# Two attentions in which one VectorE instruction adds the bias and keeps the row maximum

## The chip, the cores and the metric

The kernel runs on one core of a Trainium2 chip. The core has a matrix engine (TensorE, PE in the profile), a vector engine (VectorE, DVE), an activation engine (ScalarE, ACT), a general one (GpSimd, POOL) and SyncE (SP), which here issues loads. Each has its own queue of instructions, which it runs in order; they meet at semaphores. Data lie in SBUF; matrix products go to PSUM, here used as four banks of 128x512 (`BANK`) and two pairs of banks (`PAIR`). The metric is device time in microseconds (us).

## The reference, cut to what matters

The program is two two-layer blocks, one behind the other, for 512 tokens of width 1024. Each has an attention with 8 heads of width 64:

```python
# first block: the bias goes by the distance of query and key
scores = jnp.einsum('bclhd,bcshd->bchls', q, k_band).astype(jnp.float32) * (ATT_HEAD_DIM ** -0.5)
scores = scores + bias[None, None]
scores = jnp.where(valid[None, :, None, None, :], scores, -1e30)
p = jax.nn.softmax(scores, axis=-1).astype(v.dtype)
o = jnp.einsum('bchls,bcshd->bclhd', p, v_band)
...
# second block: normed queries and keys, a bias from the forget gates, causal
q = rms_norm(q, q_gain)
k = rms_norm(k, k_gain)
...
s = jnp.einsum('bqhd,bkhd->bhqk', qi, k).astype(jnp.float32) * scale
s = s + ci.transpose(0, 2, 1)[..., None] - ck[:, :, None, :]
s = jnp.where(kpos[None, :] <= pi[:, None], s, NEG_INF)
pr = jax.nn.softmax(s, axis=-1)
```

A softmax needs the largest score of each row, which is taken from the scores after scale and bias.

## The kernel before, in words

The whole program is one sequence per engine, written out by hand in `pe_program`, `dve_program`, `act_program`, `pool_program` and the loads of SP. No scheduler moves anything; semaphores (`bank_ready`, `bank_free`, `evac` and those of a stage) carry what depends on what. Layer normalisations, projections, two mixtures of experts, a state-space layer, an S5 layer and two feed-forward layers stand around the attentions; for their products POOL splits each weight into a high and a low part (`WH`, `WL`), and the PE runs three products.

Both attentions are the same three functions, `pe_attention`, `dve_attention` and `act_attention`; `n` is 0 for the first and 1 for the second, which the profile shows at some 190 and 1540 us. A head's scores are four row blocks `j` of 128 queries, with 128, 256, 384 and 512 keys, and lie in three banks (`HOME`). For a head `h`:

- PE, `scores(h)` (L1336, in the second attention with a product for the gates' bias, L1339): four products into three banks, each of which must have been handed back by the DVE.
- DVE, `scale(h)` (L1390): for each of the four blocks one instruction, scores times one eighth plus bias, from PSUM to `S`; the bank is handed back. Then four maxima (L1395), and their negation (L1397), which lets ACT begin.
- ACT, `exponential(h)` (L1448): four exponentials with the negated maximum as bias, and the rows' sums by the accumulator.
- DVE, `normalise(h)` (L1401, L1404): reciprocals of the sums, four products in place.
- PE, `turned(h)` (L1355): ten transposes of the probabilities; ACT copies them to `PT` (L1465); PE, `outputs(h)` (L1368): four products with V.

The DVE runs scale(0), scale(1), and then for each head normalise(h), other work, scale(h + 2). The other work is in the first attention two pieces of a matrix-vector product (`dve_ada`, L630 to L634) on weights that SP loads into `ADA_B`, and in the second `dve_s5_turning` (L3253 to L3255). Every other head it also takes the low part of two heads' outputs (`rest`, L1410). The PE runs turned(h), scores(h + 2), outputs(h). The projection behind an attention begins when the last low part is there.

The copies of the queries out of the projection are `act_copy_pairs` in the first attention, and `dve_qknorm` (L2725, with the gains `QK_GAIN`) makes those of the second; `MINUS_HEAD` is a constant with which the gates' bias is added in the PE.

## Time and profile before

| | us |
|---|---|
| median of 3 runs | 2767.97 (2766.33 to 2770.85) |
| profiled execution | 2766.05 |
| its span | 2764.1 |
| PE busy | 2495.0 (90%) |
| DVE busy | 1801.5 (65%) |
| POOL busy | 1469.9 (53%) |
| ACT busy | 964.4 (35%) |
| the 64 additions of both attentions (L1390) | 280 to 690 ns each |
| the 64 maxima (L1395) | 285 to 677 ns each |

The span is the time from the first to the last instruction of the profiled execution; the device time is a little longer. "Busy" counts the time in which an engine has at least one instruction in work. In a timeline the first number is the start in the span, the second the duration, and square brackets hold the idle time in front of it and who ended it; rows of the same line that follow one another are merged, with their count. The duration of a single instruction includes a tail in which the next one may already run, so the distance of two starts is less than the duration.

### The profile page before, as it was taken

The numbers are of one execution on the slowest core, as the hardware profiler recorded it, in microseconds if no ns is written. First come the engines' busy times: TensorE is split into PE (matmuls) and PEld (weight loads), VectorE is DVE, ScalarE is ACT, GpSimd is POOL, SyncE is SP. The second block draws the span as 40 slices with busy tenths as digits, with TensorE's granted clock in tenths as the row PEclk, the third lists the DMA queues.
The fourth block names the chain that finished last, engine by engine and source line by source line (L and its number), as shares of the span: only waits on it lengthen the run. The fifth ranks groups of instructions, "written<-read, shape, count | busy, mean of one in ns | idle before, by whom it ended". The sixth has DMA issues, their size and how long they took to land.

```text
span 2764.1 us, 36708 instructions
## 1 busy us (share of the span) xinstructions
PE 2495.0 (90%) x12718; PEld 1986.0 (72%) x12718; DVE 1801.5 (65%) x2200; ACT 964.4 (35%) x1494; POOL 1469.9 (53%) x1234
## 2 busy tenths in 40 slices
PE   4978989978999998999497789999996889999998
PEld 3754777856777776878386558888885778888887
DVE  6769866757787875667687857665137945666324
ACT  2013257742444432777312323222014631222102
POOL 4730334426555552344365126676779937666675
PEclk8977989989999998999798789999998999999999
DMA  8735569953333323899432113332241023333222
GB/s 312 261 131 205 190 241 331 325 176 92 99 99 93 98 83 116 282 337 311 141 81 80 65 54 92 105 93 89 98 125 47 32 67 94 91 103 95 95 88 84
DMA packets 319122, 386.73 MB, mean 140 GB/s; under 512 B 51578, under 2 KB 259214, under 8 KB 318902
## 3 DMA queue, kind: packets, MB, share of 16 engines
q1 hardware_dynamic: 261424, 335.84, 37.1%
q10 hardware_dynamic: 34438, 28.08, 3.3%
q0 software_dynamic: 23168, 21.59, 2.4%
q8 instruction: 57, 0.93, 0.1%
q14 instruction: 35, 0.29, 0.0%
HBM read 397.62 MB, written 55.41 MB: 164 GB/s over the span
## 4 chain that ended last, share of the span: by engine, by line
PE 35%; POOL 20%; issue 18%; DVE 14%; DMA 9%; ACT 2%; SPq 0%; ACTq 0%; POOLq 0%; DVEq 0%
POOL WL L837 14%; PE PAIR L529 6%; PE PAIR L530 5%; PE PAIR L531 5%; POOL WH L833 5%; PE PAIR L1842 4%; PE BANK L529 2%; PE BANK L530 2%; PE BANK L531 2%; DMA RAW<-in_ffn_w_up 2%; DMA RAW<-in_moe_w 2%; PE PAIR L1812 2%; DVE ADA_SUM L634 1%; PE BANK L2288 1%; DVE ADA_SUM L632 1%
## 5 line engine op out<-in xcount | busy, mean ns | idle before, releaser
L837 POOL TENSOR_TENSOR WL<-RAW,WH 128x512 fp32r<-128x512 f32 x584 | 815.1, 1426 | 12.2
L529 PE MATMUL PAIR<-HH,WH 128*128 128x512 f32 x1792 | 712.5, 398 | 56.1 <-POOL HL L1126 29.9
L530 PE MATMUL PAIR<-HL,WH 128*128 128x512 f32 x1792 | 702.6, 392 | 0.0
L531 PE MATMUL PAIR<-HH,WL 128*128 128x512 f32 x1792 | 702.1, 392 | 0.0
L832 POOL TENSOR_TENSOR TURN<-ONES 128x1 f32<-128x1 f32 x146 | 33.6, 230 | 890.0 <-PE PAIR L531 811.5
L529 PEld LDWEIGHTS PAIR<-HH,WH 128*128 128x128 f32 x1792 | 339.7, 190 | 140.9 <-issue 44.2
L530 PEld LDWEIGHTS PAIR<-HL,WH 128*128 128x128 f32 x1792 | 340.0, 190 | 71.4 <-issue 2.4
L531 PEld LDWEIGHTS PAIR<-HH,WL 128*128 128x128 f32 x1792 | 339.5, 189 | 71.8
L833 POOL TENSOR_SCALAR WH<-RAW 128x2048 fp32r<-128x2048 f32 x146 | 284.9, 1951 | 0.0
L2022 POOL DMA_INDIRECT XG<-htok_scratch,GATHER_I x78 | 107.1, 1373 | 257.3 <-PE PAIR L1812 151.3
L529 PE MATMUL BANK<-WH,GH 128*128 128x256 f32 x624 | 181.1, 290 | 0.0
L530 PE MATMUL BANK<-WL,GH 128*128 128x256 f32 x624 | 174.1, 279 | 0.0
L531 PE MATMUL BANK<-WH,GL 128*128 128x256 f32 x624 | 173.8, 279 | 0.0
L1842 PE MATMUL PAIR<-W2RAW,HT 128*128 128x512 f32 x312 | 148.0, 596 | 6.4 <-ACT HT L1884 4.7
L529 PE MATMUL PAIR<-FHH,WH 128*128 128x512 f32 x352 | 138.7, 394 | 0.0
L531 PE MATMUL PAIR<-FHH,WL 128*128 128x512 f32 x352 | 138.0, 392 | 0.0
L530 PE MATMUL PAIR<-FHL,WH 128*128 128x512 f32 x352 | 136.6, 388 | 0.0
L1949 DVE TENSOR_TENSOR WL<-RAW,WH 128x1024 fp32r<-128x1024 f32 x78 | 95.6, 1226 | 54.8 <-ACT WH L1760 54.7
L1943 DVE TENSOR_TENSOR GL<-PAIR,GH 128x1024 fp32r<-128x1024 f32 x78 | 95.5, 1224 | 50.6 <-ACT GH L1878 50.6
L2832 DVE TENSOR_TENSOR X<-PAIR,X 128x1024 f32<-128x1024 f32 x8 | 9.8, 1225 | 179.3 <-PE PAIR L531 179.3
L1812 PEld LDWEIGHTS PAIR<-IDENT,XG 128*128 128x128 f32 x624 | 83.4, 192 | 59.4 <-issue 34.3
L2794 DVE TENSOR_TENSOR PAIR<-PAIR,RSTD 128x1024 f32<-128x1024 f32 x44 | 54.2, 1232 | 109.8 <-PE PAIR L531 109.7
(530 smaller groups left out, 4841.7 us busy)
## 6 DMA issues: line engine op xcount, KB each, us to landing
RAW<-in_moe_w SPq DMA_DIRECT2D x156, 512.0 KB, 7.0
RAW<-in_ffn_w_up SPq DMA_DIRECT2D x88, 512.0 KB
W2RAW<-in_moe_w SPq DMA_DIRECT2D x78, 512.0 KB, 6.1
ADA_B<-in_ada_w SPq DMA_DIRECT2D x30, 1024.0 KB, 5.3
RAW<-in_ssm_w_in SPq DMA_DIRECT2D x48, 512.0 KB
ADA_A<-in_ada_w SPq DMA_DIRECT2D x18, 1024.0 KB, 7.7
RAW<-in_ffn_w_down SPq DMA_DIRECT2D x32, 512.0 KB
RAW<-in_ev_w_in SPq DMA_DIRECT2D x20, 512.0 KB
```

Of the source, the lines that this page charges most:

```text
L529: nc.tensor.matmul(o, wh, xh, start=start, stop=False)
L530: nc.tensor.matmul(o, wh, xl, start=False, stop=False)
L531: return nc.tensor.matmul(o, wl, xh, start=False, stop=stop)
L832: pool.tensor_tensor(TURN[:, s:s + 1], ONES[:, 0:1], ONES[:, 0:1], ALU.mult)
L833: pool.tensor_scalar(WH[:, s], RAW[:, s], 1.0, 1.0, ALU.mult, ALU.mult).then_inc(split_hi, 1)
L837: ins = pool.tensor_tensor(WL[:, s, c], RAW[:, s, c], WH[:, s, c].bitcast(F32), ALU.subtract)
L1812: ins = nc.tensor.transpose(pair[:, k // 4, (k % 4) * P:(k % 4) * P + P], rows_of(s)[:, :, k], IDENT[:])
L1842: ins = nc.tensor.matmul(pair[:, m, :], HT[:, s % 2, :], W2RAW[:, s % 2, c], start=True, stop=True)
L1943: dve.e.tensor_tensor(GL[:, s % 2].rearrange("p (b k) n -> p b (k n)", b=2), PAIR[p % 2][:], GH[:, s % 2].rearrange("p (b k) n -> p b (k n ...
L1949: dve.e.tensor_tensor(WL[:, u % 2, 0:D], RAW[:, u % 2, 0:D], WH[:, u % 2, 0:D].bitcast(F32), ALU.subtract).then_inc(w["w1_low"], 1)
L2022: pool.e.indirect_dma_start(XG[:, s % 2, :], None, htok_dram, bass.IndirectOffsetOnAxis(ap=GATHER_I[:, s:s + 1], axis=0), bounds_check=SEQ ...
L2794: dve.e.tensor_tensor(pair[:], pair[:], bcast(RSTD[:], 1, 2), ALU.mult).then_inc(w["scaled"], 1)
```

## The change

In `scale(h)` each of the four additions and the maximum of its block become one `tensor_tensor_reduce`: scores plus bias go to `S`, the largest of a row, begun from `LOWEST`, goes to `MX`. It has no factor for the scores, so the factor of one eighth goes to the queries: into ACT's copies of `Q0` in the first attention, into the gain `QK_GAIN` of the queries in the second. The bias of the gates is added in the PE before that, so `MINUS_HEAD` changes from -8 to -1. The four maxima and the wait on them go; the negation waits for the last bank's addition.

```diff
-    def act_copy_pairs(act, name, first, n, to, tokens, func=ACT.Copy):
+    def act_copy_pairs(act, name, first, n, to, tokens, func=ACT.Copy, scale=1.0):
...
-                ins = act.e.activation(to[:, 2 * i:2 * i + 2, :], pair[:], func)
+                ins = act.e.activation(to[:, 2 * i:2 * i + 2, :], pair[:], func, scale=scale)
...
-        act_copy_pairs(act, "mixin", 2, 2, Q0, False)
+        act_copy_pairs(act, "mixin", 2, 2, Q0, False, scale=HD ** -0.5)
...
-                    ins = dve.e.scalar_tensor_tensor(s[:, h % 2, SEG[j]:SEG[j] + wide], bank[:, at:at + wide],
-                                                     HD ** -0.5, bias(h)[:, SEQ - wide:SEQ], ALU.mult, ALU.add)
+                    ins = dve.e.tensor_tensor_reduce(s[:, h % 2, SEG[j]:SEG[j] + wide], bank[:, at:at + wide],
+                                                     bias(h)[:, SEQ - wide:SEQ], 1.0, LOWEST, ALU.add, ALU.max,
+                                                     MX[:, h % 2, 0, j:j + 1])
                 ins.then_inc(bank_free[b % 4], 1)
             dve.e.wait_ge(bank_free[b % 4], b // 4 + 1)
-            for j in range(NT):
-                ins = dve.e.tensor_reduce(MX[:, h % 2, 0, j:j + 1], s[:, h % 2, SEG[j]:SEG[j] + P * (j + 1)], AX.X, ALU.max)
-            dve.link(ins)
             dve.e.tensor_scalar(MX[:, h % 2, 1, :], MX[:, h % 2, 0, :], -1.0, None, ALU.mult).then_inc(w["scaled"], 1)
...
-            dve.e.tensor_scalar(MINUS_HEAD[at:at + HEADS], bcast(IDENT[0:HEADS, 0:HEADS], 2, P), -HD ** 0.5, None, ALU.mult)
+            dve.e.tensor_scalar(MINUS_HEAD[at:at + HEADS], bcast(IDENT[0:HEADS, 0:HEADS], 2, P), -1.0, None, ALU.mult)
...
+        dve.link(dve.e.tensor_scalar(QK_GAIN[:, 0:1], QK_GAIN[:, 0:1], HD ** -0.5, None, ALU.mult))
```

On the DVE, head 0 of the first attention stood so before (S the scores in SBUF, STRIP the bias, MX the maxima):

```order
L1390 SCALAR_TENSOR_TENSOR S<-BANK,STRIP 128x512 [waits bank_ready,strip_ready]
L1390 SCALAR_TENSOR_TENSOR S<-BANK,STRIP 128x384 [waits bank_ready]
L1390 SCALAR_TENSOR_TENSOR S<-BANK,STRIP 128x128
L1390 SCALAR_TENSOR_TENSOR S<-BANK,STRIP 128x256 [waits bank_ready]
L1395 TENSOR_REDUCE MX<-S 128x1 [waits bank_free0]
L1395 TENSOR_REDUCE MX<-S 128x1 x3
L1397 TENSOR_SCALAR MX<-MX 128x4 [waits dve_chain]
```

On the same engine and place it stands so now; the new instruction bears the name ISA and comes as two:

```order
L1391 ISA S,MX<-BANK,STRIP 128x512 [waits bank_ready,strip_ready]
L1391 ISA MX 128x1
L1391 ISA S,MX<-BANK,STRIP 128x384 [waits bank_ready]
L1391 ISA MX 128x1
L1391 ISA S,MX<-BANK,STRIP 128x128
L1391 ISA MX 128x1
L1391 ISA S,MX<-BANK,STRIP 128x256 [waits bank_ready]
L1391 ISA MX 128x1
L1396 TENSOR_SCALAR MX<-MX 128x4 [waits bank_free0]
```

The four maxima over 1280 columns are gone, four instructions of one column stand between the additions, and the negation waits for a bank's count.

In the second attention the DVE had this between a head's probabilities and its other work (CAUSAL is the mask):

```order
L1390 SCALAR_TENSOR_TENSOR S<-BANK,CAUSAL 128x256 [waits bank_ready]
L1395 TENSOR_REDUCE MX<-S 128x1 [waits bank_free2]
L1395 TENSOR_REDUCE MX<-S 128x1 x3
L1397 TENSOR_SCALAR MX<-MX 128x4 [waits dve_chain]
L1401 RECIPROCAL SUMS<-SUMS 128x4 [waits att1_exp]
```

And now:

```order
L1391 ISA S,MX<-BANK,CAUSAL 128x256 [waits bank_ready]
L1391 ISA MX 128x1
L1396 TENSOR_SCALAR MX<-MX 128x4 [waits bank_free2]
L1400 RECIPROCAL SUMS<-SUMS 128x4 [waits att1_exp]
```

The reciprocals that begin the next head's probabilities follow the negation as before; the four maxima no longer stand ahead of them. Nothing moves on the PE, ACT, POOL or SP.

## Rows read from the trace of the kernel before

**Rows 1.** Busy us in a stretch: length, PE, PEld, DVE, ACT, POOL, clock, DMA, GB/s

```profile
192.40:270.20 77.80, 65.84 (x227) 37.64 (x226) 72.81 (x143) 29.84 (x95) 0.00 (x0) 0.70 0.57 197
```

**Rows 2.** Waits of the DVE in each attention, summed: engine, line, waited for, us, times, longest

```profile
DVE S L1390 <- PE BANK L1336: 2.0, 4, 0.9
...
DVE S L1390 <- PE BANK L1339: 10.5, 8, 4.9
```

**Rows 3.** DVE timeline, first attention: start, duration, instruction, idle before and releaser

```profile
192.49 1.69 DVE L1390 SCALAR_TENSOR_TENSOR S<-BANK,STRIP 128x512 f32<-128x512 f32 x4
194.21 1.66 DVE L1395 TENSOR_REDUCE MX<-S 128x1 f32<-128x128 f32 x4
195.91 0.17 DVE L1397 TENSOR_SCALAR MX<-MX 128x4 f32<-128x4 f32 x1
195.98 0.68 DVE L1390 SCALAR_TENSOR_TENSOR S<-BANK,STRIP 128x512 f32<-128x512 f32 x1
197.05 1.28 DVE L1390 SCALAR_TENSOR_TENSOR S<-BANK,STRIP 128x384 f32<-128x384 f32 x3 [0.38 <-PE BANK L1336]
```

**Rows 4.** DVE groups by shape in the first attention: count, busy us, mean ns, idle before

```profile
L1390 DVE SCALAR_TENSOR_TENSOR S<-BANK,STRIP 128x512 f32<-128x512 f32 x8 | 5.5, 684 | 0.0
...
L1390 DVE SCALAR_TENSOR_TENSOR S<-BANK,STRIP 128x128 f32<-128x128 f32 x8 | 2.2, 280 | 0.0
...
L634 DVE SCALAR_TENSOR_TENSOR ADA_SUM<-ADA_B,C_ACT,ADA_SUM 128x1024 f32<-128x1024 f32 x14 | 18.0, 1285 | 0.5
```

**Rows 5.** ACT timeline, first attention: the read of an accumulator, the next exponential

```profile
196.42 0.19 ACT L1448 ACTIVATION_READ_ACCUMULATOR S<-S,MX 128x1 f32 x1
196.51 0.49 ACT L1448 ACTIVATE S<-S,MX 128x256 f32<-128x256 f32 x1
```

**Rows 6.** DVE timeline, first attention: two small instructions with a wait between them

```profile
231.80 0.17 DVE L657 TENSOR_TENSOR MOD<-BANK,COLS 128x8 f32<-128x8 f32 x1
232.00 0.18 DVE L1401 RECIPROCAL SUMS<-SUMS 128x4 f32<-128x4 f32 x1
```

**Rows 7.** PE timeline, first attention: transposes that begin heads 1, 2, 4 and 6

```profile
212.51 1.07 PE L1355 MATMUL PAIR<-IDENT,S 128*128 128x128 f32 x8 [0.41 <-issue]
...
222.57 1.97 PE L1355 MATMUL PAIR<-IDENT,S 128*128 128x128 f32 x8 [2.25 <-DVE S L1404]
...
244.25 1.24 PE L1355 MATMUL PAIR<-IDENT,S 128*128 128x128 f32 x8 [2.08 <-DVE S L1404]
...
265.42 1.90 PE L1355 MATMUL PAIR<-IDENT,S 128*128 128x128 f32 x8 [2.52 <-DVE S L1404]
```

**Rows 8.** PE timeline, second attention: transposes that begin heads 2, 3 and 5

```profile
1574.27 1.06 PE L1355 MATMUL PAIR<-IDENT,S 128*128 128x128 f32 x8 [1.78 <-issue]
...
1583.26 1.94 PE L1355 MATMUL PAIR<-IDENT,S 128*128 128x128 f32 x8 [2.43 <-issue]
...
1604.42 1.06 PE L1355 MATMUL PAIR<-IDENT,S 128*128 128x128 f32 x8 [1.62 <-issue]
```

**Rows 9.** Busy time by stretch, heads 0, 2 and 3 of the second attention

```profile
1553.30:1565.80 12.50, 12.48 (x30) 7.10 (x30) 5.68 (x16) 4.36 (x15) 0.00 (x0) 0.50 0.01 1
1574.30:1583.30 9.00, 6.57 (x31) 4.01 (x32) 8.76 (x21) 3.59 (x14) 0.00 (x0) 0.99 0.14 58
1583.30:1595.70 12.40, 12.40 (x30) 7.03 (x30) 10.07 (x23) 4.63 (x16) 0.00 (x0) 0.50 0.11 42
```

**Rows 10.** DVE timeline, second attention: additions behind head 3

```profile
1590.23 0.76 DVE L1390 SCALAR_TENSOR_TENSOR S<-BANK,CAUSAL 128x384 f32<-128x384 f32 x2 [1.44 <-PE BANK L1339]
1591.40 0.43 DVE L1390 SCALAR_TENSOR_TENSOR S<-BANK,CAUSAL 128x256 f32<-128x256 f32 x1 [0.42 <-PE BANK L1339]
```

**Rows 11.** Chain that ended last, behind the first attention: start, us, what

```profile
267.37 5.29 DMA ADA_B<-in_ada_w
```

**Rows 12.** DVE timeline, last low parts of the two attentions

```profile
278.02 1.28 DVE L1410 TENSOR_TENSOR HL<-PAIR,HH 128x512 fp32r<-128x512 f32 x2
...
1628.31 0.69 DVE L1410 TENSOR_TENSOR HL<-PAIR,HH 128x512 fp32r<-128x512 f32 x1
```

**Rows 13.** DVE timeline, ahead of the second attention

```profile
1486.48 1.48 DVE L2720 TENSOR_SCALAR VSQ<-BANK 128x512 f32<-128x512 f32 x2 [5.58 <-PE BANK L2593]
```

More of the change, by code:

```diff
@@ L27 @@
 NEG = -1e30
+LOWEST = -3e38
 UNIT = 2048
```

## The prediction

> **What bounds the kernel now.** I read the page's share by engine first, and then only the two stretches that the change touches, because an average over 2764 us says nothing about them. A stretch's busy times come first: in the first attention the DVE is busy for 72.81 of 77.80 us, the PE for 65.84, and POOL does nothing [rows 1]. So the DVE leads there, with the PE close behind. The waits of the DVE say the same: 2.0 us in the first attention, all on the PE's scores, and 10.5 us in the second, of which 4.9 fall behind head 0 [rows 2]. The PE in turn waits for the DVE's probabilities at the beginning of most heads: 0.41, 2.25, 2.08 and 2.52 us in the first attention [rows 7], 1.78, 2.43 and 1.62 in the second [rows 8]. That is the picture to keep: a ring of two engines. The DVE's probabilities let the PE turn them, the PE goes on to the scores of the head after next, and the DVE needs those for its additions. The ring runs at the pace of the DVE, and where the PE stands at its lower clock (granted 0.50, the level of 1.2 GHz) the PE has no idle time at all: 12.48 of 12.50 us, and 12.40 of 12.40 us [rows 9]. At a granted 0.99 the same work takes it 6.57 us of 9.00 [rows 9].
>
> **What is removed.** For one head the four additions take 1.69 us, from 192.49; the four maxima begin at 194.21, and their negation at 195.91: 1.70 us for the maxima, 3.42 for the whole [rows 3]. There are 16 heads in the two attentions, so 27.2 us of DVE time go. The maxima of head 0 are covered in either attention: the additions of head 1 stand still for 0.38 us behind them, because the PE still makes that head's scores [rows 3], and the second attention has the same pattern among its 8 waits [rows 2]. So 7 of 8 maxima count in each, 14 in all.
>
> **What is added.** The order of instructions shows that the new addition is two instructions, the stream over the columns and a 128x1 one that writes its result out. The stream has as many columns as the addition had. Neither it nor the small one occurs in the trace of before. *The stream:* the addition costs 280 ns at 128 columns and 684 at 512, that is 404/384 = 1.05 ns a column [rows 4]. I take the price of the addition; below that it can't be much, since the same columns come from the same places, and the upper end is a second pass over the columns, 1280 x 1.05 = 1.35 us a head. *The small one:* the nearest row is ACT's own read of its accumulator, after which the next instruction begins 0.09 us later (196.42 to 196.51) [rows 5]; I take 0.10. The lower end is what the DVE's smallest instruction holds up the next, 195.91 to 195.98, 0.07 us [rows 3]. The upper end is 0.20 us, from one small DVE instruction to a next that waits for it (231.80 to 232.00) [rows 6]. So a head saves 1.70 - 4 x 0.10 = **1.30 us**, with 1.70 - 0.28 = 1.42 and 1.70 - 0.80 = 0.90 as the ends of the small one alone.
>
> The count of DVE instructions doesn't fall: four streams, four reads and the negation are nine, as before. What goes is columns, and the rows above price columns. The Trainium skill has a rule that speaks against such a change (VectorE: DVE Perf Modes, Rules for kernel authors): don't fuse chained DVE operations for speed, lower their number. By that rule alone the sum would be nothing, 2768 us; by the rows, where a 512-column instruction costs 404 ns more than one of 128, it is the one below. The trace disagrees with the rule for instructions of this width. The time that the rule gives is that of rival (d) below.
>
> **What is moved.** The negation now waits for the last of the four pairs and not for a maximum; the wait is of the same kind and the 0.04 us in front of it stays (195.87 to 195.91) [rows 3]. Banks are handed back to the PE one small instruction later, 0.07 to 0.20 us, at a place where the PE has idle time of its own except at the lower clock. The factor of one eighth costs nothing in the copies of Q0, which are the same ACT instructions with another constant. In the second attention it is one more 128x1 DVE instruction with its wait, 0.2 us, long before a stretch in which the DVE idles 5.58 us for the PE [rows 13]; without that cover it would cost 0.2 us. The DMA queues and POOL have nothing moved.
>
> **First attention.** The PE's start of the even heads is the marker. It can't come earlier than the PE is free, so a pair of heads gains the smaller of what the DVE saves and of the PE's idle time. Head 1's maxima: 1.30. Up to head 2: 2.60 saved, idle 0.41 + 2.25 = 2.66, so 2.60. Up to head 4: idle 2.08 is smaller, so 2.08 (head 3 begins with no idle time). Up to head 6: 2.60 and the rest carried over, against 2.52, so 2.52 [rows 7]. Sum: 1.30 + 2.60 + 2.08 + 2.52 = **8.5 us**.
>
> **Second attention.** The same with the clock as it is now: 1.30 from head 1, then the idle times ahead of heads 2, 3 and 5, 1.78 + 2.43 + 1.62 = 5.83 [rows 8] (heads 1 and 4 follow stretches without any [rows 9]); 7.13 in all, under the 6 x 1.30 = 7.8 that the DVE has saved by then. The last maxima, of head 7, add 1.30 on the DVE alone: **8.4 us**.
>
> **What is late next.** Behind either attention everything hangs on the last low part, 278.02 + 1.28 us in the first and 1628.31 in the second [rows 12], and the PE's projection starts on it; no clock time is fixed there, since SP issues its loads on counts that these engines give. The one thing that could stand still is the stream of `ADA_B`: two places, each refilled in 5.29 us [rows 11] after it has been used. A piece takes the DVE two instructions of 1285 ns, 2.6 us [rows 4], and a head uses two pieces. A pair of heads lasts 21.7 us now (222.57 to 244.25 [rows 7]), so a head will last some 9.6 us, and a place that is free after 2.6 us of it is wanted again 7.0 us later. That hides the refill, by 1.7 us; without the cover each head would lose what is missing.
>
> **Sum.** 8.5 + 8.4 = 16.9 us. The profiled execution took 2766.05 us (its span is 2764.1), 1.9 under the median of 2767.97. From the median: 2767.97 - 16.9 = **2751.1 us**.
>
> **Rivals.** (a) *The clock stays up.* Less idle time on the PE may keep the upper level where it fell before. Idle times of 1.62 and 1.78 us did not bring it down, 2.43 did [rows 8, 9]. In the second attention head 3 could then run at 0.99, and the DVE's waits behind it, 1.44 + 0.42 us [rows 10], go as well: the DVE's own 7 x 1.30 + 1.86 = 11.0 instead of 8.4, so 2748.5 us. Against it: other idle stretches near 2 us remain, and the fall may only move to another head.
> (b) *The read is exposed.* At 0.20 us each a head saves 0.90, and 14 heads 12.6 us: 2755.4.
> (c) *The first attention's gain is given back* to the refills of `ADA_B` or to the loads behind them: 8.4 us are left, 2759.6. For it: the DVE already waits for one such load at the end of the attention [rows 11]. Against it: those loads begin on what the DVE has used, so they come earlier with it.
> (d) *The stream runs at half pace.* A head then saves 1.30 - 1.35 = -0.05, nothing in all: 2768.7. For it speaks that it is another instruction, with a running maximum; against it that the maxima alone cost no more per column than the additions did (1.66 and 1.69 us for the same four widths [rows 3]). The Trainium skill names such a halving (Vector Engine (DVE) Microarchitecture Reference, Points that are easy to get wrong), for the accumulating form with two sources in SBUF that aren't bf16; here one of the two sources lies in PSUM, and no trace of before has such an instruction.
> (e) *Slower:* half pace together with an exposed read. A head costs 1.35 - 0.90 = 0.45 more, 14 of them 6.3 us: 2774.3. The point from which the change costs time at all is a pair that takes 1.70/4 = 0.43 us more than the plain addition. At the lower clock the PE then also gets its banks later.
> (f) That the change doesn't do what it says is excluded as far as the instructions go: their order has the reductions gone and the pairs in their place.
>
> **How the numbers follow.** Forecast 0.45, (a) 0.22, (b) 0.10, (c) 0.07, (d) 0.09, (e) 0.07. The range of 2745 to 2763 holds the first four, 0.84; its lower end takes (a) with the cheapest read, 0.12 x 14 = 1.7 us below 2748.5, and a little for a second head that keeps its clock; its upper end takes (c) with the exposed read, some 3 us above 2759.6. (d) and (e), 0.16, are left out. A measurement of this kernel can tell about 0.2%, 5.5 us, from no change: faster by more holds for the first four, 0.84; within it lies (d), 0.09; (e) is slower, 0.07.
>
> **What would show it.** The maxima's 1.66 us groups are gone. The streams last 0.28 to 0.69 us; 1.1 us or more at 512 columns would mean (d). From the first stream of a head without waits to the negation should be 2.1 us; 2.5 would mean (b). The PE's idle time ahead of heads should be under 0.6 us for the even heads of the first attention. A granted clock of 0.9 or more at head 3 of the second attention would be (a). The last low parts should end 8.5 us and 16.9 us earlier; a distance that shrinks between the two attentions would be (c). I am wrong if the pair costs over 0.3 us more than the addition, or if the ring is held by something that the DVE's waits don't show.

## The result, and the profile after

The changed kernel takes 2745.1 us (2741.4 to 2747.1), the kernel before 2767.3 beside it: a ratio of 0.9914, 95% interval 0.9898 to 0.9930. Two more measurements of the same kernel gave 2743.2 (0.9910, 0.9896 to 0.9924) and 2745.4 (0.9917, 0.9901 to 0.9932); the last of these medians holds one execution of 7063 us at a granted clock of 0.35, which its ratio leaves out, and is 2744.7 without it. So it is faster, by 22 to 24 us where 16.9 were forecast. By that ratio the kernel takes 2744.2 us where the one before takes 2767.97, which is 0.8 us below the range. The direction and the place were right, the size was not.

Where the time went is best seen by cutting both traces at the same instructions. An attention is counted from its first addition to the end of its last low part; the projection behind the second attention from there to the first residual.

| us, by the profiled executions | before | after | after, second | after, third |
|---|---|---|---|---|
| whole execution | 2766.05 | 2747.09 | 2741.99 | 2746.13 |
| first attention | 86.81 | 75.13 | 75.09 | 77.32 |
| first attention's end to the end of the first mixture of experts | 334.38 | 338.71 | 335.07 | 333.56 |
| from there to the second attention | 929.24 | 926.79 | 926.57 | 929.30 |
| second attention | 86.08 | 72.63 | 72.45 | 72.56 |
| projection behind it | 11.38 | 13.69 | 13.58 | 13.67 |
| from there to the end of the feed-forward stage | 1054.38 | 1054.42 | 1054.34 | 1054.38 |
| end stage | 71.29 | 72.63 | 72.61 | 72.67 |

By the first of them the two attentions give 11.7 + 13.5 = 25.1 us. The second attention takes the same 72.5 us in all three, but the first doesn't: 75.1, 75.1 and 77.3 us. Two places behind them lose in each of the three: the projection 2.3 and the end stage 1.4. The stretch of the first mixture of experts lies between 334 and 339 us in executions of one and the same program, so one profile can't say whether the change moves it; the same holds for the 927 to 929 us behind it.

The DVE timeline of the first attention after the change (start, duration, instruction, idle before and releaser), which answers to [rows 3]:

```profile
193.09 0.69 DVE L1391 CUSTOM_DVE_ANT_0 S<-BANK,STRIP 128x512 f32<-128x512 f32 x1
193.71 0.08 DVE L1391 DVE_READ_ACCUMULATOR2_ANT MX<- 128x1 f32 x1
193.71 0.55 DVE L1391 CUSTOM_DVE_ANT_0 S<-BANK,STRIP 128x384 f32<-128x384 f32 x1
...
194.40 0.42 DVE L1391 CUSTOM_DVE_ANT_0 S<-BANK,STRIP 128x256 f32<-128x256 f32 x1
...
194.86 0.17 DVE L1396 TENSOR_SCALAR MX<-MX 128x4 f32<-128x4 f32 x1
195.96 0.69 DVE L1391 CUSTOM_DVE_ANT_0 S<-BANK,STRIP 128x512 f32<-128x512 f32 x1 [0.93 <-PE BANK L1337]
...
197.66 0.56 DVE L1391 CUSTOM_DVE_ANT_0 S<-BANK,STRIP 128x384 f32<-128x384 f32 x1 [1.01 <-PE BANK L1337]
```

The stream takes what the addition took: 0.69 us at 512 columns, 0.42 at 256. The read of the accumulator shows 0.08 us, but the next stream begins at the same time as it, 193.71: it delays nothing. From the first stream to the negation there are 194.86 - 193.09 = 1.77 us, before 3.42 [rows 3]. A head saves **1.65 us**, not 1.30; of the 1.70 us of the maxima, 0.05 are spent again. Head 0's share is covered, as forecast: the waits in head 1's additions grew from 0.38 us [rows 3] to 0.93 + 1.01.

Busy time by stretch after (length, PE, PEld, DVE, ACT, POOL, granted clock, DMA share, GB/s): the first attention, the second, and of the second heads 0 and 3.

```profile
193.10:268.20 75.10, 64.75 (x250) 37.09 (x248) 67.43 (x152) 31.73 (x100) 0.00 (x0) 0.78 0.70 241
1533.70:1606.30 72.60, 57.66 (x228) 34.52 (x228) 60.14 (x165) 31.20 (x100) 0.00 (x0) 0.85 0.25 91
1542.40:1554.20 11.80, 11.77 (x31) 6.84 (x31) 5.00 (x17) 4.68 (x16) 0.00 (x0) 0.53 0.09 30
1568.10:1576.10 8.00, 6.57 (x31) 4.02 (x31) 7.74 (x22) 4.07 (x15) 0.00 (x0) 1.00 0.16 66
```

Head 3 of the second attention ran at 0.50 and took 12.40 us [rows 9]; now it runs at 1.00 and takes 8.0. Head 0 is still at the lower level of 1.2 GHz. The same two stretches of before, as PE rows (length, PE busy, granted clock, DMA share, GB/s), show what level the PE had over a whole attention:

```profile
192.40:279.30 86.90, 71.96 (x250) 0.72 0.59 207
1542.90:1629.00 86.10, 67.70 (x228) 0.75 0.21 77
```

The count of matmuls is the same, 250 and 228, but the PE needs 7.2 us less for them in the first attention (5.8 and 5.4 less in the two other profiles) and 10.0 less in the second, because more of them run at 2.4 GHz: 0.72 became 0.78, 0.75 became 0.85.

The PE timeline after, the transposes that begin a head: four heads of the first attention (2, 3, 4 and 6), then heads 3 and 4 of the second. They answer to [rows 7, 8].

```profile
219.66 1.07 PE L1356 MATMUL PAIR<-IDENT,S 128*128 128x128 f32 x8
227.27 1.06 PE L1356 MATMUL PAIR<-IDENT,S 128*128 128x128 f32 x8 [1.67 <-issue]
238.27 1.07 PE L1356 MATMUL PAIR<-IDENT,S 128*128 128x128 f32 x8
253.75 1.97 PE L1356 MATMUL PAIR<-IDENT,S 128*128 128x128 f32 x8 [1.20 <-DVE S L1403]
...
1568.09 1.07 PE L1356 MATMUL PAIR<-IDENT,S 128*128 128x128 f32 x8 [0.77 <-issue]
1576.08 1.06 PE L1356 MATMUL PAIR<-IDENT,S 128*128 128x128 f32 x8 [1.43 <-issue]
```

In the first attention heads 2 and 4 began behind 2.25 and 2.08 us of idle time and at a lower level (1.97 and 1.24 us for the same eight transposes [rows 7]); in this execution they begin without any, at 1.07. Which heads of the first attention fall differs between executions: in the second profile of the same kernel head 2 begins at 1.97 us behind 1.23 us of idle time. A head can also begin at the upper level and fall right behind, as head 3 here. From its first transpose to the next head's (length, PE busy, granted clock, DMA share, GB/s):

```profile
227.20:238.30 11.10, 11.03 (x43) 0.69 0.61 220
```

In the second attention every head from 1 on runs at the upper level throughout (1.00 in each stretch). The waits of the DVE on scores there, the sum and the last of them:

```profile
DVE S L1391 <- PE BANK L1340: 10.6, 8, 4.9
...
1557.94 0.56 DVE L1391 CUSTOM_DVE_ANT_0 S<-BANK,CAUSAL 128x384 f32<-128x384 f32 x1 [0.30 <-PE BANK L1340]
```

The sum is the old one, 10.6 after 10.5 [rows 2], and misleads: head 0's covered maxima now stand in it as waiting, 1.5 us more, while nothing is waited for behind 1557.94. The waits of 1.44 and 0.42 us behind head 3 [rows 10] are gone.

What was lost is on the PE behind the second attention, where the projection starts. The PE timeline of before:

```profile
1629.22 0.47 PE L529 MATMUL PAIR<-HH,WH 128*128 128x512 f32 x1 [3.54 <-issue]
1629.98 0.39 PE L529 MATMUL PAIR<-HH,WH 128*128 128x512 f32 x1
```

And of after:

```profile
1606.56 0.76 PE L530 MATMUL PAIR<-HH,WH 128*128 128x512 f32 x1 [5.13 <-issue]
1607.98 0.63 PE L530 MATMUL PAIR<-HH,WH 128*128 128x512 f32 x1
...
1611.65 0.40 PE L530 MATMUL PAIR<-HH,WH 128*128 128x512 f32 x1
```

The PE now finishes its last outputs early and waits 5.13 us, not 3.54, for the last low part, which on the DVE stands behind the last block of another task (`dve_s5_turning(dve, KD - 1)`, then `rest(3)`). The projection then runs its first 5.1 us at 0.63 us a matmul instead of 0.39, at a granted clock of 0.52. The end stage, 8 us of it from 48 us behind its start (length, PE busy, clock, DMA share, GB/s), and the first matmul behind the wait in it, of before:

```profile
2742.76:2750.76 8.00, 5.25 (x24) 1.00 0.00 0
2748.32 0.51 PE L529 MATMUL PAIR<-PH,WH 128*128 128x512 f32 x1 [2.75 <-POOL WL L837]
```

Of after:

```profile
2722.46:2730.46 8.00, 5.25 (x19) 0.82 0.00 0
2728.02 0.80 PE L530 MATMUL PAIR<-PH,WH 128*128 128x512 f32 x1 [2.75 <-POOL WL L838]
```

The wait is 2.75 us in both, and yet the clock stays at 1.00 in one and falls to 0.82 in the other. So the 1.4 us are the clock again, but the length of the idle time alone doesn't say whether it falls. Nor does the change: with the new instruction in one attention only, in either, that first matmul takes 0.50 us and the end stage 71.2 us.

### The profile page after: what moved, and what is told of

Same layout as the page of the kernel before. It is cut to its first block, busy times and chain, and to the rows that moved or that the text cites. A ratio compares the mean times of both kernels' runs of the same rounds, so it can differ in the third digit from the quotient of the medians.

```text
span 2745.2 us, 36709 instructions
## 1 busy us (share of the span) xinstructions
PE 2483.8 (90%) x12718; PEld 1982.0 (72%) x12718; DVE 1775.0 (65%) x2201; ACT 964.4 (35%) x1494; POOL 1473.7 (54%) x1234
## 4 chain that ended last, share of the span: by engine, by line
PE 34%; POOL 21%; issue 19%; DVE 13%; DMA 9%; ACT 2%; SPq 0%; ACTq 0%; POOLq 0%; DVEq 0%
POOL WL L838 15%; PE PAIR L530 6%; POOL WH L834 5%; PE PAIR L531 5%; PE PAIR L532 5%; PE PAIR L1841 4%; DMA RAW<-in_moe_w 3%; PE BANK L530 2%; PE BANK L531 2%; PE BANK L532 2%; PE PAIR L1811 2%; PE BANK L2287 1%; DVE ADA_SUM L635 1%; DMA ADA_B<-in_ada_w 1%; DMA RAW<-in_ffn_w_up 1%
```

## The experiments

The theory behind the first runs: the gain is the DVE's columns, plus some 2 us in the second attention because the PE's clock stays up, less what the clock takes back behind it. The rival: the gain beyond the forecast has another source than the DVE's columns (places in memory, the order, the loads).

**The change again, and one attention at a time.** Edit of the last two: the new instruction for one value of `n`, and the old two for the other, the factor of one eighth going with it.

```
-                    ins = dve.e.tensor_tensor_reduce(...)
+                    if n == 0:      # second_only: n == 1
+                        ins = dve.e.tensor_tensor_reduce(...)
+                    else:
+                        ins = dve.e.scalar_tensor_tensor(...)
...
+            if n != 0:
+                for j in range(NT):
+                    ins = dve.e.tensor_reduce(MX[:, h % 2, 0, j:j + 1], ...)
```

> The changed kernel unaltered, for its ratio and a second trace. Theory T (columns saved at 1.65 us a head because the read hides, 7 heads in each attention, plus some 2 us in the second attention where the PE's clock no longer falls, less what the clock gives back at the projection behind it): 20 to 24 us faster than before. If the 2.3 us at the projection was chance, the first product behind the second attention does not fall to 1.2 GHz again. Rival L (a plain linear sum, 14 x 1.65 = 23.1 us, clock irrelevant): 23 us.

> Only the first attention has the new instruction (queries scaled there alone); the second is as before. T and L: the first attention ends 11.5 us earlier (7 x 1.65). If loads behind it take part of that back, as rival (c) of the prediction says, the whole is faster by 7 to 9 us and the end of the first mixture of experts stands less than 11 us earlier; if not, by 11 us.

> Only the second attention has the new instruction (gain of the queries and the constant of the gates' bias scaled for it); the first is as before. T: the attention is 13.5 us shorter (7 x 1.65 = 11.5, and 2 us of waits behind head 3, where the clock stays up), and the projection gives 2 us back if the clock falls there: 11 to 13.5 us faster in all. L: 11.5 us, with head 3 still at 1.2 GHz.

Beside 2766.9 for the kernel before: 2743.2; the first attention alone 2757.5 (0.9963, 0.9950 to 0.9976), the second alone 2752.1 (0.9943, 0.9928 to 0.9958). That is 9.4 and 14.8 us, together 24.2, against 23.7 for both: within the intervals, which are some 4 us to either side, the gains add up. The first alone shows the second attention at 86.06 us and the projection at 11.39, as before. The second alone shows the projection at 13.08: the loss there belongs to the second attention's own change.

Neither came as expected. The first attention was to end 11.5 us earlier and lasts 78.01 us in its profile, 8.8 less than before; from its end to the second attention there are 1262.6 us, before 1263.6, so nothing is given back behind it. What is missing lies inside. The DVE's own time in the first attention, its length less the DVE's waits, is 83.1 us before and 69 to 69.5 in the eight profiles whose first attention has the new instruction and nothing else changed. Eight heads of 1.65 us are 13.2 of it. But the waits were 3.7 us before, and are 5.6, 5.8 and 8.1 in the changed kernel's profiles and 9.0 here. Most of the difference is a single load of `ADA_B` early in the attention. By the DVE timeline, of the changed kernel's first and third profile:

```profile
203.01 1.28 DVE L633 SCALAR_TENSOR_TENSOR ADA_SUM<-ADA_B,C_ACT,ADA_SUM 128x1024 f32<-128x1024 f32 x1 [0.48 <-DMA ADA_B<-in_ada_w]
...
206.10 1.28 DVE L633 SCALAR_TENSOR_TENSOR ADA_SUM<-ADA_B,C_ACT,ADA_SUM 128x1024 f32<-128x1024 f32 x1 [3.99 <-DMA ADA_B<-in_ada_w]
```

Seven of the eight lengths are 75.1 to 78.0 us and one is 83.2, so the first attention gained 8.8 to 11.7 us in most executions and 3.6 in one; the first profile shows the upper end. The second alone gained 14.8 us where 11 to 13.5 were expected: its attention lasts 69.86 us, because head 0's transposes and outputs took 8.2 us there and not 11.8, with the same instructions.

**The maxima kept beside the new instruction.** The four reductions are done again behind the streams, so the columns are all there, and so is the new instruction.

```
+            for j in range(NT):
+                ins = dve.e.tensor_reduce(MXDUP[:, j:j + 1], s[...], AX.X, ALU.max)
+            dve.link(ins)
```

> The changed kernel, with the four maxima of each head taken once more, as before, into a spare tile that nobody reads (extra work). It differs from the kernel before only in the new instruction with its read in place of the addition. T and L: the gain is columns alone, so nothing is left of it: within 1.5 us of before, some 14 x 0.05 = 0.7 us slower. If the gain came from the waits that went with the maxima, part of it stays, 3 us or more.

> The changed kernel, with one maximum over 512 columns put back in each head of the second attention, into a spare tile that nobody reads: 0.60 us from start to start plus its wait, 0.64, in 7 heads that count. L: 4.5 us slower than the changed kernel, 18 us faster than before. T: the PE's idle time ahead of heads grows from at most 1.44 to some 2.1 us; if that brings the clock down in one head, another 2 us go and the attention is 6.5 us longer; if the clock holds, 4.5.

2779.7 us (1.0038, 1.0025 to 1.0051), 12.8 slower than before, which neither theory had; and with a single maximum of 512 columns in the second attention's heads 2762.5 (0.9975, 0.9964 to 0.9985). Their traces were longer in places that have nothing to do with an attention: the feed-forward stages 395.45 to 397.8 and 658.9 to 663 or 664 us. Both have one more tile of 16 bytes, `MXDUP`. So one run had that tile alone, never used, and two had the repeated maxima without it, written over `MX`, which holds the same numbers.

> The changed kernel with a tile of 16 bytes a partition allocated ahead of QK_GAIN that no instruction uses; only addresses move. Theory M (the 7 us that kept_maxima and one_maximum lost in the feed-forward stages come from the moved addresses): 7 us slower than the changed kernel, 2.4 us of it between the first evout residual and the end of the first feed-forward layer, 4 to 5 up to the end of the second. Rival: that loss came from the instructions added; then no change from the changed kernel.

> The maxima taken once more, as in kept_maxima, but written over the same values in MX, so that no new tile moves the addresses of the others. Theory T: with the DVE's work of before back in each head, both attentions are as long as before, 86 to 88 us each, the feed-forward stages are as in the kernel before, and the whole is within 1.5 us of before. Rival V (the new instruction itself costs something that its own rows don't show): 5 us or more slower than before, as kept_maxima was.

> One maximum over 512 columns put back in each head of the second attention, written over the same value in MX, with no new tile. T: that attention is 4.5 us longer than in the changed kernel by the DVE's time alone, and 6 to 6.5 if the PE's idle time, which grows past 2 us, brings the clock down in one head, as it did in one_maximum; the whole 4.5 to 7 us over the changed kernel.

The tile alone costs 12 to 14 us: 2757.7 (0.9960, 0.9945 to 0.9974) where the changed kernel takes 2743 to 2745. Three of the groups of its page (line, engine, operation, count, busy us, mean ns, idle before):

```profile
L533 PE MATMUL PAIR<-FHH,WL 128*128 128x512 f32 x352 | 140.4, 399 | 0.0
L532 PE MATMUL PAIR<-FHL,WH 128*128 128x512 f32 x352 | 138.7, 394 | 0.0
L531 PE MATMUL PAIR<-FHH,WH 128*128 128x512 f32 x352 | 138.0, 392 | 0.0
```

The same three of the changed kernel:

```profile
L530 PE MATMUL PAIR<-FHH,WH 128*128 128x512 f32 x352 | 138.7, 394 | 0.0
L532 PE MATMUL PAIR<-FHH,WL 128*128 128x512 f32 x352 | 138.0, 392 | 0.0
L531 PE MATMUL PAIR<-FHL,WH 128*128 128x512 f32 x352 | 136.6, 388 | 0.0
```

Compared by their operands, two of the groups are 6 and 7 ns a matmul slower and the third (FHH, WH) 2 ns faster: 3.8 us more of busy time over 1056 matmuls, and 2.4 + 4.0 = 6.4 us in the length of the two stages. The 2.4 us stand in all three kernels with the tile and in no other. The second stage is less firm: it takes 658.9 us in most profiles without the tile, but 660.5 us in three, and 662.0 in the run that follows. Why a shift by 16 bytes does that wasn't found. Part of the rest lies in the stretch of the first mixture of experts: 339.8 to 341.8 us in the three kernels with the tile, 333.6 to 338.7 in the others.

Without the tile the test says what it was made for. With all maxima kept: 2771.0 (1.0013, 1.0004 to 1.0022), 3.3 us slower than before and not within the expected 1.5, the attentions 87.87 and 87.52 us, the second feed-forward stage 3.1 us longer in its profile. Its first head on the DVE:

```profile
192.53 0.69 DVE L1391 CUSTOM_DVE_ANT_0 S<-BANK,STRIP 128x512 f32<-128x512 f32 x1
...
194.30 1.67 DVE L1397 TENSOR_REDUCE MX<-S 128x1 f32<-128x128 f32 x4
196.00 0.17 DVE L1399 TENSOR_SCALAR MX<-MX 128x4 f32<-128x4 f32 x1
```

From the first stream to the negation 3.47 us, against 3.42 before and 1.77 in the changed kernel. With the columns back, all of the gain is gone: it was the DVE's columns, and the clock's part hangs on them. With one maximum of 512 columns in each head of the second attention the kernel takes 2752.7 us (0.9941, 0.9927 to 0.9956), and that attention 77.37 instead of 72.5 us: 4.9 where seven such maxima of 677 ns make 4.7. The clock falls again at head 4, which was to cost 1.5 to 2 us more; but head 0 took 8.9 us in this profile and not 11.8, and that hides it. So the 4.9 don't show the price of columns alone. By the medians the kernel takes 7.6 to 9.5 us more than the changed one, where 4.5 to 7 were expected. Head 4, by the PE timeline:

```profile
1577.19 1.48 PE L1356 MATMUL PAIR<-IDENT,S 128*128 128x128 f32 x8 [2.15 <-issue]
```

**The clock alone, in the kernel before.** Dummy 128x128 products of the identity with itself keep the PE at work while it waits for the probabilities in the second attention: twelve ahead of heads 2, 3, 5 and 6, and in a later run five ahead of each head but the first.

```
+            if n == 1 and h in (2, 3, 5, 6):   # later: n == 1 and h
+                for _ in range(12):            # later: 5
+                    nc.tensor.matmul(bank[:, 2 * P:3 * P], IDENT[:], IDENT[:], start=True, stop=True)  # later: 3 * P:4 * P
             pe.wait(w["probs"])
```

> The kernel before with 12 products of the identity with itself (extra work, into half a bank that nobody uses) on the PE ahead of its wait for the probabilities, in heads 2, 3, 5 and 6 of the second attention. The DVE's work is untouched. T: with its idle time filled the PE keeps the upper level in head 3, and the DVE's waits behind that head (0.17 + 1.44 + 0.42 us) go: 2 us faster. L, or if filling doesn't hold the clock: no change, head 3 still at 0.50.

> The kernel before, with five dummy 128x128 products of the identity with itself, into a bank's unused quarter, ahead of the wait for the probabilities in every head but the first of the second attention. Theory, that some 2 us of the second attention's gain in the changed kernel are DVE's waits behind head 3, which are there because TensorE falls to its lower level of clock in that head: no head from 1 on shows 2 us for its transposes, DVE's waits of 1.44 and 0.42 us behind head 3 are gone, this attention takes about 84 us instead of 86.1, and the kernel is 2 us faster unless the projection behind it falls to the lower level (1.5 to 2.3 us slower, then no change). Rival, that those waits have another cause: they stay, and the attention takes 86 us.

The first: 2768.7 (0.9999, 0.9988 to 1.0011). Head 3 keeps its level, but the fall moves to head 4, and to the projection:

```profile
1585.11 1.04 PE L1358 MATMUL PAIR<-IDENT,S 128*128 128x128 f32 x8
1593.66 1.81 PE L1358 MATMUL PAIR<-IDENT,S 128*128 128x128 f32 x8 [2.01 <-issue]
...
1628.27 0.76 PE L529 MATMUL PAIR<-HH,WH 128*128 128x512 f32 x1 [5.13 <-issue]
```

The attention gains 1.7 us and the projection loses 1.5. The second: every head from 1 on begins with at most 1.09 us for its transposes. The DVE timeline has its last waits for scores already behind head 1:

```profile
1569.87 0.69 DVE L1393 SCALAR_TENSOR_TENSOR S<-BANK,CAUSAL 128x512 f32<-128x512 f32 x1 [0.64 <-PE BANK L1339]
1570.90 1.09 DVE L1393 SCALAR_TENSOR_TENSOR S<-BANK,CAUSAL 128x384 f32<-128x384 f32 x3 [0.34 <-PE BANK L1339]
```

The waits behind head 3 are gone, the attention takes 84.56 us (84 was expected), the projection keeps its 11.38. What the fall in head 3 cost in the kernel before is thus 1.5 us, by the trace. Head 6 began at 1.09 us too, but fell right behind and ran at 0.60 (before at 0.53), so it is not the price of all the falls. The median of 2766.5 (1.0000, 0.9991 to 1.0009) can't show it; the expected 2 us were within what a measurement of this kernel can't tell.

**The low part issued early.** The last low part is put ahead of the last block of the other task, and, in a second version, dummy products fill the PE's wait.

```
+        rest(HEADS // 2 - 1)
         if n:
             dve_s5_turning(dve, KD - 1)
-        rest(HEADS // 2 - 1)
```

> The changed kernel with the last low part taken ahead of the last turning table in the second attention, instead of behind it. That part is ready at about 1602.1 us of the trace and is taken at 1605.66; the table then runs while the PE is at the projection. 2.5 to 3 us faster than the changed kernel by the DVE's order alone, and, if the shorter idle time of the PE keeps its clock up at the projection, another 2 us: 2738 to 2743. If the projection is not what decides there, no change.

> The same, and 14 products of the identity with itself (extra work, into half a bank that nobody uses) behind the last outputs, where the PE waits for the last low part. T: the projection begins at 2.4 GHz, 2.3 us faster than where the clock falls there, and no gain over the kernel without them where it doesn't fall. If the products delay the projection, up to 1 us slower.

> The changed kernel with the last low part taken early (rest_early), 9 products of the identity with itself (extra work, into a part of a bank that nobody reads) ahead of the first wait for probabilities in each attention and 14 behind the last outputs in each. T: head 0 of either attention comes to the upper level sooner, 1 to 3 us each, and the products behind both attentions begin at it, 1.7 and 2.3 us: 5 to 8 us faster than rest_early, 2735 to 2739. If the clock doesn't go by the idle time in front, no faster than rest_early.

The PE timeline at the start of the projection, with the low part early:

```profile
1602.64 0.47 PE L530 MATMUL PAIR<-HH,WH 128*128 128x512 f32 x1 [1.64 <-issue]
```

And with 14 dummy products behind the last outputs as well, the dummies and then the start:

```profile
1597.70 3.39 PE L1383 MATMUL BANK<-IDENT 128*128 128x128 f32 x28
1600.85 0.47 PE L530 MATMUL PAIR<-HH,WH 128*128 128x512 f32 x1
```

With the low part early the wait is 1.64 us instead of 5.13, the projection begins at the upper level and takes 11.82 us, and the second attention 69.1. So 1.9 of the 2.3 us lost behind the attention are the clock: that step is shown. The 0.4 left stay open. Yet the median is 2743.4 (0.9908, 0.9887 to 0.9928), no better than the changed kernel; a feed-forward stage was 1.7 us longer in its profile, and the rest of the missing 5 us isn't explained. With 14 dummies the median is 2739.3 (0.9894, 0.9872 to 0.9915), but the projection takes 13.28 us although its clock is up: the dummies outlast the wait. With nine dummies ahead of head 0 and 14 behind the last outputs, in both attentions and again with the low part early, it is 2740.8 (0.9905, 0.9890 to 0.9921), where 2735 to 2739 were expected. There head 0 of the second attention begins at the upper level and the attention takes 65.80 us. In the first attention nothing is gained: 78.18 us, where 75.1 to 78.0 are common without dummies, and head 0's transposes begin 1.6 us later than without.

**Both at once, without waste.** The low part early, and six dummies ahead of head 0 of the second attention only, beside the changed kernel on the same chip.

> The changed kernel with rest(3), the last low part of each attention, issued ahead of TensorE's last outputs (as in the run that did only that: second attention 69.11 us, projection stage 11.82 us, 2743.35 us), and six dummy 128x128 products of the identity with itself, into a bank's unused quarter, ahead of the wait for the probabilities in the second attention's head 0. Theory, that the time of this attention beyond DVE's columns is the granted clock of TensorE, which follows how long TensorE stood idle: head 0's transposes and outputs run at the upper level (transposes about 1.0 us instead of 2.0), the second attention takes 65 to 67 us, the projection behind it stays near 11.8 us, and the kernel takes 2738 to 2741 us. Rival, that head 0's time is set by DVE and ACT alone: the attention stays at 69 us and the kernel within 2 us of 2743.

> The changed kernel once more, on the chip of the two others. By both earlier medians 2742 to 2746 us, the second attention 72.5 us, the projection stage 13.6 us. Theory and rival say the same here: it is what the other two are read against.

2737.5 us (0.9888, 0.9874 to 0.9902) beside 2744.7: 7.2 us less, 0.5 below the expected 2738 to 2741. The second attention takes 64.96 us and the projection 11.84. Head 0's dummies and its transposes:

```profile
1543.03 2.72 PE L1351 MATMUL BANK<-IDENT 128*128 128x128 f32 x12
1545.59 1.04 PE L1359 MATMUL PAIR<-IDENT,S 128*128 128x128 f32 x8
```

This is the lowest median of the kernels run, though its interval overlaps those of the two before it (0.9894 and 0.9905). In the same profile the first attention was 83.2 us long, though its instructions are those of the changed kernel: in the first attention the last low part stands where it stood. By its timeline the DVE waited three times for longer than 2 us, on a load, on ACT's copies of the transposes and on ACT's copies of the outputs:

```profile
209.61 1.28 DVE L633 SCALAR_TENSOR_TENSOR ADA_SUM<-ADA_B,C_ACT,ADA_SUM 128x1024 f32<-128x1024 f32 x1 [5.28 <-DMA ADA_B<-in_ada_w]
...
267.55 0.17 DVE L658 TENSOR_TENSOR MOD<-BANK,COLS 128x8 f32<-128x8 f32 x1 [2.52 <-ACT PT L1467]
...
277.41 0.69 DVE L1412 TENSOR_TENSOR HL<-PAIR,HH 128x512 fp32r<-128x512 f32 x1 [2.35 <-ACT HH L1455]
```

The first wait, at head 0, is 4.8 us longer than in the changed kernel's first profile. The two others stand behind a fall of the clock: the PE began head 5 at 1.06 us behind 2.31 us of idle time, and from 258 to 272 us its granted clock was 0.50. That gave back 6 to 8 us in one execution. In four more of the eight profiles the same wait is 3.0 to 4.0 us.

## Why the prediction was right or wrong

**The price of the new instruction: wrong by 0.35 us a head, on the good side.** The stream's price, that of the addition, was right to 0.01 us. The first step that failed is "the nearest row is ACT's own read of its accumulator [...]; I take 0.10". The DVE's read delays no stream; the four of a head cost 0.05 us together, not 0.40. The lower end of 0.07 was no lower end either: with it a head would have saved 1.42 us, and it saved 1.65. Under the other steps as they stood, this alone is worth 1.1 us: 1.65 + 2.66 + 2.08 + 2.52 = 8.9 in the first attention and 1.65 + 5.83 + 1.65 = 9.1 in the second, 18.0 instead of 16.9.

**The ceiling by the PE's idle time: this is the step that cost most.** "It can't come earlier than the PE is free, so a pair of heads gains the smaller of what the DVE saves and of the PE's idle time." In the second attention the list of idle times was not complete. It has heads 2, 3 and 5; the longest stands ahead of head 6, by the PE timeline of before:

```profile
1614.07 1.94 PE L1355 MATMUL PAIR<-IDENT,S 128*128 128x128 f32 x8 [3.08 <-issue]
```

With these 3.08 us the idle time is more than the DVE saves up to there, so the ceiling binds nothing and the step gives 7 x 1.30 = 9.1 us, not 8.4. With the true price of the read it gives 7 x 1.65 = 11.55. What is still missing is the clock: the waits behind head 3, 1.44 + 0.42 = 1.86 us, were taken as fixed and are gone. That makes 13.4, and 13.5 to 13.6 were measured in three profiles. For the clock's part there is a run: with head 3 held at its level in the kernel before, the attention was 1.5 us shorter.

In the first attention the ceiling isn't refuted in the same way. With the true price of the read it gives 8.9 us; measured were 8.8 to 11.7 us in seven of eight profiles, and 9.4 by the median of the kernel with that attention alone. The sign that was given, an idle time under 0.6 us ahead of the even heads, held in the first profile for heads 2 and 4 (none) and not for head 6 (1.20). In the changed kernel's three profiles the PE needed 5.4 to 7.2 us less for the same 250 matmuls, so its idle time, read from a trace in which it ran partly at 1.2 GHz, was no fixed limit. That this is what made the room is argued; nothing here holds the clock down. Against it stood the loads of `ADA_B`.

**The total owes something to luck.** With these corrections the sum is 8.9 + 13.4 = 22.3 us, and 22 to 24 were measured. But no sum has the projection's loss of 2.3 us; in the total it is covered by what the first attention gained beyond 8.9, up to 2.8 us.

**Rival (a), the clock stays up,** had the right mechanism for the second attention and the right 1.86 us, and 0.22 of the chance. With the true price of the read its sum there is the measured one. Its last sentence also held: the fall moved, out of head 3 and into the projection. What that would cost was not worked out, and is 2.3 us there.

**The first maxima are covered:** right, by the waits in head 1's additions (0.38 us before, 0.93 + 1.01 after).

**What is late next.** The last low parts stand where the text looked:

```profile
266.94 1.28 DVE L1409 TENSOR_TENSOR HL<-PAIR,HH 128x512 fp32r<-128x512 f32 x2
...
1605.66 0.69 DVE L1409 TENSOR_TENSOR HL<-PAIR,HH 128x512 fp32r<-128x512 f32 x1
```

They come 11.1 and 22.7 us earlier than [rows 12], not 8.5 and 16.9. The distance grows between the attentions, so rival (c) as a whole is out. But the margin of 1.7 us did not hide the loads. The DVE's waits for `ADA_B` in the first attention after the change, the sum, how often and the longest:

```profile
DVE ADA_SUM L633 <- DMA ADA_B<-in_ada_w: 3.1, 4, 0.9
```

They had been 1.2 us in all, and are 3.8 and 6.0 us in the two other profiles. A head lasts 75.13/8 = 9.4 us now, for which the prediction's own working still gives a margin of some 1.5 us; why single loads come later than that wasn't traced.

**Rivals (b), (d) and (e)** are out by the streams' own rows: no exposed read and no half pace. The sentences of the Trainium skill that the prediction weighed fare as follows. "VectorE: DVE Perf Modes", Rules for kernel authors, advises against fusing for speed: two instructions into one (and a read) saved 1.65 us a head here at the same count of nine instructions, and instructions of 128 to 512 columns cost 0.28 to 0.69 us, by the column. "Vector Engine (DVE) Microarchitecture Reference", Points that are easy to get wrong, has a halved pace of the accumulating form for two sources in SBUF that aren't bf16; with one source in PSUM these rows show none.

**The range.** Its lower end of 2745 took rival (a) with "the cheapest read" and a little for one more head. With the read at nothing and no ceiling in either attention, 2767.97 - 11.55 - 13.4 = 2743.0 would have been an end of it, and the result inside.

## What to carry to other kernels

Before idle time is used as a ceiling, list it for every head, the last ones too. And where the granted clock of the idling engine changes within the trace, its idle time is no fixed ceiling: with a faster partner it may keep its level and be free earlier, so take both clock cases through every stage that the change touches, and through the wait behind it. Price a result that an instruction keeps beside its stream at nothing as one end of the range, and price columns, not instructions, where they are some hundreds wide. Take the length of a stage from several profiles before its parts are matched to tenths of a microsecond. In an experiment that adds a tile, run the tile alone too, or write into one that is there.

## What the runs showed of the hardware

- The DVE's read of its accumulator shows 0.08 us and delays nothing: the next 128x384 stream has the same start, 193.71.
- The granted clock of the PE and the idle time ahead of it: after 0.77, 1.43 and 1.64 us it stayed at the upper level; after 2.15 and 5.13 us it was lower (1.48 us for the transposes, 0.76 for the first matmul). In between it went either way. After 1.73 us a head ran at 1.00 and after 1.74 us another at 0.60, in one profile; after 2.75 us it stayed at 1.00 or fell to 0.82 in neighbouring kernels; head 6 of the first attention took 1.97 or 1.09 us for its transposes behind the same 1.20 us, in two profiles. Idle time alone doesn't decide.
- The clock can fall right behind transposes that still show 1.06 us: behind 1.67 us of idle time a head began so and had 0.69 over its 11.1 us. The first instruction of a head doesn't tell its level.
- Head 0 of the second attention took 11.7 us in some profiles and 8.2 in others, with the same instructions (1542.04 to 1553.75 in one, 1541.08 to 1549.28 in another), and so moves the length of that attention by 2 to 3 us by itself.
- One load of 1024 KB into `ADA_B` kept the DVE waiting for 0.5 us in some executions and for 3.0 to 5.3 us in others, with the same instructions around it.
- An unused SBUF tile of 16 bytes a partition made 1056 matmuls 3.8 us longer in sum (704 of them 6 or 7 ns slower each, 352 of them 2 ns faster) and the kernel 12 to 14 us slower. The effect is larger than half of the change under study.
